# The gated embedding stage with products of rounded parts, its weights in ten pieces, and its transposes between the halves of the gate product

## The chip, the cores and the metric

The kernel runs on one core of one Trainium2 chip. The metric is the device time of one execution in microseconds (us), here the median of three. TensorE does matrix products, VectorE and ScalarE elementwise work, GpSimd the gathers, and SyncE issues DMAs.

## The reference

The whole computation is a decoder block with a mixture of experts, followed by a second block. The change touches one stage between them, the gated embedding ("ple"). There, x has 1024 rows (tokens) of 1024, p has 1024 rows of 256, `w_ple_gate` is 1024 x 1024 and `w_ple_proj` 256 x 1024, all float32:

```python
x = x + hierarchical_moe(...)
ple_gate = jax.nn.sigmoid(rms_norm(x, norm_ple[l]) @ w_ple_gate[l])
x = x + ple_gate * (p[l] @ w_ple_proj[l])
```

The sum with the experts' output is part of the stage too: each token gathers its two expert rows and adds them, weighed, to x.

## The kernel before

The kernel is a row of phases with a barrier between them. Within a phase each engine has its own instruction list, and the lists meet only at semaphores. Each list runs in its written order, so an instruction that waits holds up everything behind it on its engine.

The stage goes over eight tiles of 128 tokens. `each_tile` writes tile 0 and tile 7 out and puts tiles 1 to 6 in a loop of two tiles a pass; buffers with `b` are used in turn. What happens to tile t:

- GpSimd (L855) gathers the two expert rows of each token, `yb`, two tiles ahead.
- SyncE loads `xt` (L823) and `pt` (L824) into buffer b. The load of tile t+2 stands behind the store of tile t (L828), and the store waits for `added` of tile t.
- VectorE `weigh` (L893): adds the two weighed expert rows to `xt`. `norm`: ScalarE squares and sums (L865), VectorE takes the mean (L901), ScalarE the root (L867), VectorE the reciprocal (L904) and `h`, the scaled rows (L907).
- TensorE `turn` (L940, L943): eight transposes of h and two of pt into PSUM banks 0 to 2.
- VectorE `copy`: pT (L912), and hT with the gain (L913).
- TensorE `product` (L949) twice: the gate (eight steps of 128 rows by two halves of 512 columns, banks 4 and 5) and the projection (two steps by two halves, banks 6 and 7). Both in plain float32, which the profile shows as two records for each product. A product is "halved" by output columns: `h` is the outer loop, `k` the inner one.
- ScalarE takes the sigmoid of the gate's sums (L874). VectorE multiplies it with the projection (m, L922) and adds xt (y, L925); that sets `added`.

The orders in the lists matter here. In the step for tile t, TensorE does the gate product of t, `turn` of t+1, and the projection of t (which waits for `added` of t-1). VectorE does `norm` and `copy` of t+1, and then m and y of t. ScalarE does the square and root of t+1, then the sigmoid of t. All weights are fetched once, the gate's in one DMA of 4 MB (L835) and the projection's in one of 1 MB (L837); TensorE waits for both before the first product.

The other stages that the prediction draws on: "mix" mixes the branches, with plain products (L736) and transposes (L717) of the same shapes; "fin" is the last stage, whose products already go in rounded parts (L1122), with weights rounded on ScalarE (L1067) and the remainders on VectorE (L1104).

## Time and profile before

| | |
|---|---|
| three runs | 3751.92, 3756.41, 3767.01 us |
| median | 3756.41 us |
| profiled execution, its own time | 3761.07 us |
| its span, first to last instruction | 3759.3 us |
| mean granted clock of TensorE | 0.894 of full |
| the stage's first DMA issue | 2167.85 us |
| first transpose | 2188.16 us |
| first product of the gate | 2196.60 us |
| first transposes of tiles 1, 2, 7 | 2212.63, 2231.82, 2328.00 us |
| end of the last y | 2352.55 us |
| next stage's first DMA issue | 2356.23 us |

Times inside the profile count from the start of the span. A view of the timeline gives start, duration, engine, line, operation, output and inputs, how many instructions are merged in the row, and in brackets how long the engine was idle before it and what ended that. "PE" is TensorE's product or transpose. Products are pipelined: the duration of one record is longer than the distance from one start to the next, so distances of starts are what counts. The granted clock is given as a share of 2.4 GHz.

### The profile page before, as it was taken

The numbers are of one execution on the slowest core, as the hardware profiler recorded it, in microseconds if no ns is written. First come the engines' busy times: TensorE is split into PE (matmuls) and PEld (weight loads), VectorE is DVE, ScalarE is ACT, GpSimd is POOL, SyncE is SP. The second block draws the span as 40 slices with busy tenths as digits, with TensorE's granted clock in tenths as the row PEclk, the third lists the DMA queues.
The fourth block names the chain that finished last, engine by engine and source line by source line (L and its number), as shares of the span: only waits on it lengthen the run. The fifth ranks groups of instructions, "written<-read, shape, count | busy, mean of one in ns | idle before, by whom it ended". The sixth has DMA issues, their size and how long they took to land. (4 is left out here: it accounts for less than half of the span.)

```text
span 3759.3 us, 53218 instructions
## 1 busy us (share of the span) xinstructions
PE 3102.9 (83%) x20841; PEld 2514.8 (67%) x20841; DVE 1870.1 (50%) x2424; ACT 1196.4 (32%) x1698; POOL 684.5 (18%) x363
## 2 busy tenths in 40 slices
PE   7999948888686998399999969799998946635699
PEld 6999937777453444388888734699998745533387
DVE  3003726666363223588888723300576745566421
ACT  2000014333353111377777612201111642222310
POOL 3232224332000000222222110222221411100000
PEclk9999978888697998699999989899998967766899
DMA  4223231110203521599999742434566230021321
GB/s 169 79 98 131 106 106 45 44 47 8 77 12 139 191 101 55 205 389 399 399 399 399 291 169 78 173 104 154 177 225 211 100 137 0 0 88 33 140 95 63
DMA packets 247611, 548.22 MB, mean 146 GB/s; under 512 B 29776, under 2 KB 90576, under 8 KB 246368
## 3 DMA queue, kind: packets, MB, share of 16 engines
q1 hardware_dynamic: 198208, 431.01, 31.9%
q10 hardware_dynamic: 39376, 80.81, 5.8%
q0 software_dynamic: 9872, 34.23, 2.4%
q8 instruction: 109, 1.79, 0.2%
q14 instruction: 46, 0.38, 0.0%
HBM read 430.32 MB, written 114.50 MB: 145 GB/s over the span
## 5 line engine op out<-in xcount | busy, mean ns | idle before, releaser
L359 PE MATMUL pin_psum<-pin_sb_w,pin_sb_hT 128*128 128x354 f32 (+1 forms) x5376 | 974.7, 343 | 23.0 <-DVE pin_sb_w L321 18.0
L359 PEld LDWEIGHTS pin_psum<-pin_sb_w,pin_sb_hT 128*128 128x128 f32 x5376 | 935.7, 189 | 59.0 <-DVE pin_sb_w L321 18.8
L3827 DVE TENSOR_TENSOR moe_sb_wlo<-moe_sb_raw,moe_sb_whi 128x2048 fp32r<-128x2048 f32 x192 | 437.9, 2287 | 93.3 <-ACT moe_sb_whi L3652 93.2
L3652 ACT ACTIVATE moe_sb_whi<-moe_sb_raw 128x2048 fp32r<-128x2048 f32 x192 | 367.3, 1916 | 134.6 <-DMA moe_sb_raw<-in_w_gate 48.9
L338 DVE TENSOR_SCALAR pin_sb_xt<-pin_psum,pin_sb_ss 128x353 f32<-128x353 f32 (+1 forms) x112 | 69.3, 625 | 496.6 <-PE pin_psum L359 496.4
L293 ACT ACTIVATE pin_sb_xt<-pin_psum,pin_sb_ss 128x353 f32<-128x353 f32 (+1 forms) x112 | 64.0, 589 | 563.6 <-PE pin_psum L359 560.2
L3895 PE MATMUL moe_psum<-moe_sb_whi,moe_sb_xhi 128*128 128x512 f32 x512 | 204.6, 400 | 15.9 <-DVE moe_sb_xlo L3831 15.9
L3895 PE MATMUL moe_psum<-moe_sb_wlo,moe_sb_xhi 128*128 128x512 f32 x512 | 201.3, 393 | 0.0
L3895 PE MATMUL moe_psum<-moe_sb_whi,moe_sb_xlo 128*128 128x512 f32 x512 | 201.3, 393 | 0.0
L250 POOL CAST pin_sb_w<-pin_sb_raw 128x2832 fp32r<-128x2832 f32 (+1 forms) x26 | 75.6, 2908 | 642.8 <-PE pin_psum L359 596.3
L252 POOL TENSOR_TENSOR pin_sb_w<-pin_sb_raw,pin_sb_w 128x2832 fp32r<-128x2832 f32 (+1 forms) x26 | 185.6, 7139 | 3.9 <-issue 0.6
L3895 PEld LDWEIGHTS moe_psum<-moe_sb_whi,moe_sb_xhi 128*128 128x128 f32 x512 | 97.3, 190 | 41.3 <-issue 19.1
L3626 POOL COPY moe_sb_idx<-moe_sb_idx_all 128x1 int32 (+1 forms) x32 | 50.9, 1592 | 381.1 <-PE moe_psum L3884 378.9
L949 PE MATMUL ple_psum<-ple_sb_wg,ple_sb_hT 128*128 128x512 f32 x256 | 113.5, 602 | 6.1 <-DMA ple_sb_wp<-in_w_ple_proj 6.1
L736 PE MATMUL mix_psum<-mix_sb_wo,mix_sb_mT 128*128 128x512 f32 x256 | 113.1, 600 | 0.0
L3895 PEld LDWEIGHTS moe_psum<-moe_sb_whi,moe_sb_xlo 128*128 128x128 f32 x512 | 97.3, 190 | 20.8
L3895 PEld LDWEIGHTS moe_psum<-moe_sb_wlo,moe_sb_xhi 128*128 128x128 f32 x512 | 97.3, 190 | 19.4
L3895 PE MATMUL moe_psum<-moe_sb_whi,moe_sb_ahi 128*128 128x512 f32 x256 | 103.4, 404 | 6.4 <-DVE moe_sb_alo L3835 6.4
L1122 PE MATMUL fin_psum<-fin_sb_whi,fin_sb_mhi 128*128 128x512 f32 x256 | 101.3, 396 | 6.0 <-DVE fin_sb_mlo L1080 6.0
L3895 PE MATMUL moe_psum<-moe_sb_whi,moe_sb_alo 128*128 128x512 f32 x256 | 101.2, 395 | 0.0
L3895 PE MATMUL moe_psum<-moe_sb_wlo,moe_sb_ahi 128*128 128x512 f32 x256 | 101.1, 395 | 0.0
L1122 PE MATMUL fin_psum<-fin_sb_wlo,fin_sb_mhi 128*128 128x512 f32 x256 | 100.6, 393 | 0.0
(668 smaller groups left out, 5553.7 us busy)
## 6 DMA issues: line engine op xcount, KB each, us to landing
moe_sb_raw<-in_w_gate SPq DMA_DIRECT2D x64, 1024.0 KB, 13.9
moe_sb_raw<-in_w_up SPq DMA_DIRECT2D x64, 1024.0 KB, 14.1
moe_sb_raw<-in_w_down SPq DMA_DIRECT2D x64, 1024.0 KB, 13.1
pin_sb_raw<-in_w_in SPq DMA_DIRECT2D x16, 1412.0 KB, 8.0
scratch_proj<-pin_sb_xt ACTq DMA_DIRECT2D x16, 1412.0 KB, 7.0
pin_sb_raw<-in_w_in SPq DMA_DIRECT2D x12, 1792.0 KB, 7.8
scratch_proj<-pin_sb_xt ACTq DMA_DIRECT2D x12, 1792.0 KB, 6.3
scratch_ybuf<-moe_sb_yb ACTq DMA_DIRECT2D x32, 512.0 KB, 6.8
```

Of the source, the lines that this page charges most:

```text
L250: pool.tensor_copy(wt[b][0][:, :, :], raw[b][:, :, :])
L252: pool.tensor_tensor(wt[b][1][:, :, :], raw[b][:, :, :], wt[b][0][:, :, :].bitcast(F32), ALU.subtract)\
L293: a.activation(og[b][:, t, :], ps[:, t, 0:width], ACT.Copy, scale=ss[:, 3, t:t + 1]).then_inc(act_free, 1)
L338: v.tensor_scalar(og[b][:, t, :], ps[:, t, 0:width], ss[:, 3, t:t + 1], None, ALU.mult).then_inc(dve_free, 1)
L359: mm = te.matmul(ps[:, t, 0:cols], hT[a_part][:, k, t * P:(t + 1) * P], wt[b][w_part][:, k, :], start=(k == 0 and n == 0), stop=(k == KD - ...
L736: mm = te.matmul(ps[:, 6 + n, :], mT[:, k, :], wo[:, k, n * 512:(n + 1) * 512], start=(k == 0), stop=(k == KD - 1))
L949: mm = te.matmul(ps[:, bank + h, :], a[:, k, :], w[:, k, h * 512:(h + 1) * 512], start=(k == 0), stop=(k == n_k - 1))
L1122: mm = te.matmul(ps[:, 4 + 2 * b + h, :], m[:, k, :], w[:, k, h * 512:(h + 1) * 512], start=(k == 0 and i == 0), stop=(k == KM - 1 and i = ...
L3626: pool.tensor_copy(idx[b][:, :], idx_all[:, bass.ds(n, 1)] if not isinstance(n, int) else idx_all[:, n:n + 1])
L3652: s.activation(whi[q][:, :, :], raw[q][:, :, :], ACT.Copy).then_inc(hi, 1)
L3827: tt(wlo[q][:, :, :], raw[q][:, :, :], whi[q][:, :, :].bitcast(F32), ALU.subtract).then_inc(lo, 1)
L3895: mm = te.matmul(out, xp[:, k, :], wp[q][:, w_at, :], start=(first and i == 0), stop=(last and i == 2))
```

## The change

Four edits, all in this stage:

- Every product a @ w becomes three, hi(a) hi(w) + hi(a) lo(w) + lo(a) hi(w), in the rounded format float32r. hi is the value rounded to that format, lo what remains. The rows' hi parts are made by ScalarE (`round_rows`), after VectorE's gain (`gained`); the lo parts by VectorE after that. The same tiles are double-buffered.
- The weights arrive in ten pieces of 128 rows (eight of the gate, two of the projection), each with a semaphore, ahead of the load of tile 1. ScalarE rounds each piece (`round_weights`), VectorE takes the remainder (`rest_of_weights`): six of them ahead of the norm of tile 0, four behind it.
- For tile 0 the gate product goes by k, each step waiting for its piece.
- From tile 1 on, `turn` of the next tile stands between the two halves of the gate product instead of behind it.

```diff
@@ -786,11 +786,12 @@
 
 
 
+    KW, LEAD = KD + 2, 6
     with Phase(nc, "ple") as ph:
         ident = ph.sb("ident", [P, P])
         gcol = ph.sb("gcol", [P, KD])
-        wg = ph.sb("wg", [P, KD, D])
-        wp = ph.sb("wp", [P, 2, D])
+        raw = ph.sb("raw", [P, KW, D])
+        whi, wlo = (ph.sb(n, [P, KW, D], F32R) for n in ("whi", "wlo"))
         two = lambda n, shape: [ph.sb(f"{n}{b}", shape) for b in range(2)]
         xt = two("xt", [P, D])
         pt = two("pt", [P, 2, P])
@@ -798,7 +799,8 @@
         ss = two("ss", [P, 4])
         h = ph.sb("h", [P, D])
         hT = ph.sb("hT", [P, KD, P])
-        pT = two("pT", [P, 2, P])
+        hThi, hTlo = ([ph.sb(f"{n}{b}", [P, KD, P], F32R) for b in range(2)] for n in ("hThi", "hTlo"))
+        pThi, pTlo = ([ph.sb(f"{n}{b}", [P, 2, P], F32R) for b in range(2)] for n in ("pThi", "pTlo"))
         sg = ph.sb("sg", [P, D])
         m = ph.sb("m", [P, D])
         y = two("y", [P, D])
@@ -806,12 +808,14 @@
         wts = ph.sb("wts", [P, 2, NT])
         yb = [[ph.sb(f"yb{b}{k}", [P, D]) for k in range(2)] for b in range(2)]
         ps = ph.psum()
-        const_in, table_in, wg_in, wp_in = (ph.sem(n) for n in ("const_in", "table_in", "wg_in", "wp_in"))
+        const_in, table_in, w_hi, w_lo = (ph.sem(n) for n in ("const_in", "table_in", "w_hi", "w_lo"))
+        w_in = [ph.sem(f"w_in{k}") for k in range(KW)]
         y_in = [ph.sem(f"y_in{b}") for b in range(2)]
         weighed = ph.count("weighed")
         x_in, y_st = ([ph.sem(f"{n}{b}") for b in range(2)] for n in ("x_in", "y_st"))
-        squared, mean, root, normed, turned, copied, gate_sums, proj_sums, gates, added = (ph.count(n) for n in (
-            "squared", "mean", "root", "normed", "turned", "copied", "gate_sums", "proj_sums", "gates", "added"))
+        squared, mean, root, normed, turned, gained, rounded, copied, gate_sums, proj_sums, gates, added = (
+            ph.count(n) for n in ("squared", "mean", "root", "normed", "turned", "gained", "rounded", "copied",
+                                  "gate_sums", "proj_sums", "gates", "added"))
         blk = ph.block()
 
         @blk.sync
@@ -832,9 +836,10 @@
             load(0, 0)
             for dst, src in ((ident[:, :], g["ident"]), (gcol[:, :], g["norm_ple"].rearrange("(k p) -> p k", p=P))):
                 sp.dma_start(dst, src, allow_slow_non_contiguous=True).then_inc(const_in, 16)
-            sp.dma_start(wg[:, :, :], g["w_ple_gate"].rearrange("(k p) n -> p k n", p=P)).then_inc(wg_in, 16)
+            for k in range(KW):
+                src = g["w_ple_gate"][k * P:(k + 1) * P, :] if k < KD else g["w_ple_proj"][(k - KD) * P:(k - KD + 1) * P, :]
+                sp.dma_start(raw[:, k, :], src).then_inc(w_in[k], 16)
             load(1, 1)
-            sp.dma_start(wp[:, :, :], g["w_ple_proj"].rearrange("(k p) n -> p k n", p=P)).then_inc(wp_in, 16)
             with sp.Fori(0, NT // 2 - 1) as j:
                 for b in range(2):
                     store(2 * j + b, b)
@@ -866,16 +871,31 @@
                 s.wait_ge(mean.sem, mean.done(t))
                 s.activation(ss[b][:, 2:3], ss[b][:, 1:2], ACT.Sqrt).then_inc(root.sem, 1)
 
+            def round_rows(t, b):
+                s.wait_ge(gained.sem, gained.done(t))
+                s.activation(hThi[b][:, :, :], hT[:, :, :], ACT.Copy)
+                s.activation(pThi[b][:, :, :], blocks(ps, 2, 2), ACT.Copy).then_inc(rounded.sem, 1)
+
+            def round_weights(k):
+                s.wait_ge(w_in[k], 16)
+                s.activation(whi[:, k, :], raw[:, k, :], ACT.Copy).then_inc(w_hi, 1)
+
             def body(t, b, n):
                 if not last(t):
                     norm(t + 1, 1 - b, n + b)
+                    round_rows(t + 1, 1 - b)
                 s.wait_ge(gate_sums.sem, gate_sums.done(t))
                 s.wait_ge(added.sem, added.done(t - 1))
                 s.activation(sg[:, :], banks(ps, 4), ACT.Sigmoid).then_inc(gates.sem, 1)
 
-            for c in (squared, root, gates):
+            for c in (squared, root, rounded, gates):
                 c.begin(s)
+            for k in range(LEAD):
+                round_weights(k)
             norm(0, 0, 0)
+            for k in range(LEAD, KW):
+                round_weights(k)
+            round_rows(0, 0)
             each_tile(s, body)
 
         @blk.vector
@@ -909,8 +929,15 @@
             def copy(t, b, n):
                 ve.drain()
                 ve.wait_ge(turned.sem, turned.done(t))
-                ve.tensor_copy(pT[b][:, :, :], blocks(ps, 2, 2))
-                tt(hT[:, :, :], blocks(ps, 0, 8), bcast(gcol[:, :], P), ALU.mult).then_inc(copied.sem, 1)
+                tt(hT[:, :, :], blocks(ps, 0, 8), bcast(gcol[:, :], P), ALU.mult).then_inc(gained.sem, 1)
+                ve.drain()
+                ve.wait_ge(rounded.sem, rounded.done(t))
+                tt(hTlo[b][:, :, :], hT[:, :, :], hThi[b][:, :, :].bitcast(F32), ALU.subtract)
+                tt(pTlo[b][:, :, :], blocks(ps, 2, 2), pThi[b][:, :, :].bitcast(F32), ALU.subtract).then_inc(copied.sem, 1)
+
+            def rest_of_weights(k):
+                ve.wait_ge(w_hi, k + 1)
+                tt(wlo[:, k, :], raw[:, k, :], whi[:, k, :].bitcast(F32), ALU.subtract).then_inc(w_lo, 1)
 
             def body(t, b, n):
                 if not last(t):
@@ -924,11 +951,15 @@
                 ve.wait_ge(y_st[b], 16 * n + 16)
                 tt(y[b][:, :], xt[b][:, :], m[:, :], ALU.add).then_inc(added.sem, 1)
 
-            for c in (mean, normed, copied, added, weighed):
+            for c in (mean, normed, gained, copied, added, weighed):
                 c.begin(ve)
+            for k in range(LEAD):
+                rest_of_weights(k)
             ve.wait_ge(const_in, 32)
             ve.wait_ge(table_in, 32)
             norm(0, 0, 0)
+            for k in range(LEAD, KW):
+                rest_of_weights(k)
             copy(0, 0, 0)
             each_tile(ve, body)
 
@@ -943,28 +974,44 @@
                     mm = te.transpose(block_of(ps, 2, i), pt[b][:, i, :], ident[:, :])
                 mm.then_inc(turned.sem, 1)
 
-            def product(bank, a, w, n_k):
-                for h in range(2):
-                    for k in range(n_k):
-                        mm = te.matmul(ps[:, bank + h, :], a[:, k, :], w[:, k, h * 512:(h + 1) * 512],
-                                       start=(k == 0), stop=(k == n_k - 1))
+            def product(bank, a, b, k0, n_k, h, k):
+                hi, lo = a
+                for i, (m, w) in enumerate(((hi[b], whi), (hi[b], wlo), (lo[b], whi))):
+                    mm = te.matmul(ps[:, bank + h, :], m[:, k, :], w[:, k0 + k, h * 512:(h + 1) * 512],
+                                   start=(k == 0 and i == 0), stop=(k == n_k - 1 and i == 2))
                 return mm
+
+            gate_rows, proj_rows = (hThi, hTlo), (pThi, pTlo)
 
             def body(t, b, n):
                 te.wait_ge(copied.sem, copied.done(t))
                 te.wait_ge(gates.sem, gates.done(t - 1))
-                product(4, hT, wg, KD).then_inc(gate_sums.sem, 1)
-                if not last(t):
+                if first(t):
+                    for k in range(KD):
+                        te.wait_ge(w_lo, k + 1)
+                        for h in range(2):
+                            mm = product(4, gate_rows, b, 0, KD, h, k)
+                    mm.then_inc(gate_sums.sem, 1)
+                    te.wait_ge(w_lo, KW)
                     turn(t + 1, 1 - b, n + b)
+                else:
+                    for k in range(KD):
+                        product(4, gate_rows, b, 0, KD, 0, k)
+                    if not last(t):
+                        turn(t + 1, 1 - b, n + b)
+                    for k in range(KD):
+                        mm = product(4, gate_rows, b, 0, KD, 1, k)
+                    mm.then_inc(gate_sums.sem, 1)
                 te.wait_ge(added.sem, added.done(t - 1))
-                product(6, pT[b], wp, 2).then_inc(proj_sums.sem, 1)
+                for h in range(2):
+                    for k in range(2):
+                        mm = product(6, proj_rows, b, KD, 2, h, k)
+                mm.then_inc(proj_sums.sem, 1)
 
             for c in (turned, gate_sums, proj_sums):
                 c.begin(te)
             te.wait_ge(const_in, 32)
             turn(0, 0, 0)
-            te.wait_ge(wg_in, 16)
-            te.wait_ge(wp_in, 16)
             each_tile(te, body)
```

## Rows read from the trace of the kernel before

**Rows 1.** Stretches from transpose to transpose, tiles 1 to 7: busy us (records) by engine, clock, DMA

```profile
2231.82:2250.91 19.09, 18.48 (x51) 8.57 (x51) 7.64 (x9) 5.34 (x7) 1.88 (x2) 1.00 0.34 116
...
sum 115.37, PE 110.83 PEld 51.34 DVE 45.85 ACT 29.45 POOL 7.52; mean PE 18.47 PEld 8.56 DVE 7.64 ACT 4.91 POOL 1.25
```

**Rows 2.** Timeline of TensorE in the stage.

```profile
2212.63 1.04 PE L940 MATMUL ple_psum<-ple_sb_ident,ple_sb_h 128*128 128x128 f32 x8
...
2217.16 13.90 PE L949 MATMUL ple_psum<-ple_sb_wg,ple_sb_hT 128*128 128x512 f32 x32
2231.82 1.10 PE L940 MATMUL ple_psum<-ple_sb_ident,ple_sb_h 128*128 128x128 f32 x8 [0.77 <-DVE ple_sb_h L907]
...
2232.97 3.60 PE L949 MATMUL ple_psum<-ple_sb_wp,ple_sb_pT 128*128 128x512 f32 x8
...
2250.91 1.09 PE L940 MATMUL ple_psum<-ple_sb_ident,ple_sb_h 128*128 128x128 f32 x8 [0.61 <-DVE ple_sb_h L907]
```

**Rows 3.** Timeline of VectorE, tile 1's m and y to tile 3's h.

```profile
2236.68 1.22 DVE L922 TENSOR_TENSOR ple_sb_m<-ple_sb_sg,ple_psum 128x1024 f32<-128x1024 f32 x1 [1.95 <-PE ple_psum L949]
2238.06 1.23 DVE L925 TENSOR_TENSOR ple_sb_y<-ple_sb_xt,ple_sb_m 128x1024 f32<-128x1024 f32 x1 [0.16 <-issue]
...
2244.39 1.28 DVE L893 SCALAR_TENSOR_TENSOR ple_sb_xt<-ple_sb_yb,ple_sb_wts,ple_sb_xt 128x1024 f32<-128x1024 f32 x1 [5.11 <-DMA ple_sb_pt<-in_p]
...
2248.34 0.15 DVE L901 TENSOR_SCALAR ple_sb_ss<-ple_sb_ss 128x1 f32<-128x1 f32 x1 [1.22 <-ACT ple_sb_junk L865]
...
2250.10 0.75 DVE L907 TENSOR_SCALAR ple_sb_h<-ple_sb_xt,ple_sb_ss 128x1024 f32<-128x1024 f32 x1
```

**Rows 4.** Timeline of TensorE, the last stage's first products in rounded parts.

```profile
3555.80 0.80 PE L1122 MATMUL fin_psum<-fin_sb_whi,fin_sb_mhi 128*128 128x512 f32 x1 [6.04 <-DVE fin_sb_mlo L1080]
...
3559.70 0.39 PE L1122 MATMUL fin_psum<-fin_sb_whi,fin_sb_mhi 128*128 128x512 f32 x1
...
3562.42 0.39 PE L1122 MATMUL fin_psum<-fin_sb_whi,fin_sb_mhi 128*128 128x512 f32 x1
```

**Rows 5.** Timeline of TensorE, a restart in the mixing stage.

```profile
1468.47 1.97 PE L717 MATMUL mix_psum<-mix_sb_ident,mix_sb_h 128*128 128x128 f32 x8 [3.27 <-DVE mix_sb_h L657]
1470.23 15.79 PE L736 MATMUL mix_psum<-mix_sb_wo,mix_sb_mT 128*128 128x512 f32 x32
```

**Rows 6.** Stretch of that restart.

```profile
1468.47:1474.00 5.53, 5.53 (x13) 3.44 (x14) 1.23 (x1) 0.00 (x0) 0.00 (x0) 0.50 0.23 95
```

**Rows 7.** Instructions of the last stage's weight tile: ns min/median/max, first and last start, forms.

```profile
L1067 ACT ACTIVATE fin_sb_whi<-fin_sb_y x4: 1047/1056/1061, 3540.9 to 3557.3; 128x1024 fp32r<-128x1024 f32 x4
L1104 DVE TENSOR_TENSOR fin_sb_wlo<-fin_sb_y,fin_sb_whi x4: 1216/1222/1225, 3541.9 to 3559.1; 128x1024 fp32r<-128x1024 f32 x4
```

**Rows 8.** Groups by line in the stage: busy us, mean ns, idle before, what ended it.

```profile
L913 DVE TENSOR_TENSOR ple_sb_hT<-ple_psum,ple_sb_gcol 128x1024 f32<-128x1024 f32 x8 | 9.7, 1214 | 0.0
...
L874 ACT ACT_TABLE_LOAD x7 | 9.0, 1283 | 1.3 <-PE ple_psum L949 1.3
...
L874 ACT ACTIVATE ple_sb_sg<-ple_psum 128x1024 f32<-128x1024 f32 x8 | 8.2, 1027 | 30.5 <-PE ple_psum L949 30.4
...
L912 DVE COPY ple_sb_pT<-ple_psum 128x256 f32<-128x256 f32 x8 | 3.4, 424 | 25.5 <-PE ple_psum L943 25.5
```

**Rows 9.** Groups by line of ScalarE: a copy of 256 columns from PSUM.

```profile
L1959 ACT ACTIVATE att_sb_qkT<-att_psum 128x256 f32<-128x256 f32 x28 | 10.5, 376 | 0.0
```

**Rows 10.** Timeline of the opening, VectorE and TensorE.

```profile
2181.63 2.66 DVE L893 SCALAR_TENSOR_TENSOR ple_sb_xt<-ple_sb_yb,ple_sb_wts,ple_sb_xt 128x1024 f32<-128x1024 f32 x2 [27.01 <-DMA ple_sb_yb<-scratch_ybuf,ple_sb_di]
...
2187.26 0.75 DVE L907 TENSOR_SCALAR ple_sb_h<-ple_sb_xt,ple_sb_ss 128x1024 f32<-128x1024 f32 x1
...
2196.60 16.19 PE L949 MATMUL ple_psum<-ple_sb_wg,ple_sb_hT 128*128 128x512 f32 x32 [6.07 <-DMA ple_sb_wp<-in_w_ple_proj]
```

**Rows 11.** Stretch of the opening.

```profile
2185.00:2190.00 5.00, 1.84 (x9) 1.87 (x10) 1.07 (x3) 1.96 (x4) 1.44 (x2) 0.50 1.02 409
```

**Rows 12.** Timeline of the stage's end, TensorE and VectorE.

```profile
2328.00 1.09 PE L940 MATMUL ple_psum<-ple_sb_ident,ple_sb_h 128*128 128x128 f32 x8 [0.80 <-DVE ple_sb_h L907]
...
2351.32 1.23 DVE L925 TENSOR_TENSOR ple_sb_y<-ple_sb_xt,ple_sb_m 128x1024 f32<-128x1024 f32 x1
```

## The prediction, made before the changed kernel ran

> **What bounds the stage now.** The change touches one stage, the gated embedding, so I read that stage alone. First the stretches view, cut at the first transpose of each tile: six tile turns take 115.37 us, 19.23 us each, at full clock (1.00, 2.4 GHz), and TensorE is recorded busy for 110.83 of them [rows 1]. That looks like a TensorE bound, and a cheaper product would then pay in full. The timeline says otherwise. After 13.90 us of gate product TensorE still waits 0.6 to 0.9 us in every turn before it can transpose, and VectorE's h is what it waits for [rows 2]. So I followed h back on VectorE [rows 3]: the multiply m of tile t-1 starts at 2236.68, y ends at 2239.29, then comes a wait of 5.11 us for a DMA (SyncE reloads xt and pt of tile t+1 into the buffers of t-1, and does so only behind the store of y, which waits for `added`), then the two weighing operations, the mean, the root, and h (start 2250.10, 0.75 us). The transpose follows at 2250.91. The ring is: transposes, projection product, m, y, reload, weighing, norm, transposes of the next tile. Its two parts are
>
> - from the first transpose to m: 2231.82 to 2236.68, 4.86 us (1.15 us of ten transposes, 3.43 of projection, 0.28 of the last product's tail and hand-over) [rows 2, 3];
> - from m to the next first transpose: 2250.91 - 2236.68 = 14.23 us; over the six turns 19.23 - 4.85 = 14.38 us. I use 14.38.
>
> The gate product (32 records a tile, 2217.16 to the end of the queue at about 2230.9) lies beside the second part, and covers it all but those 0.6 to 0.9 us. It is not in the ring. The ring is what the change must be priced on.
>
> **Part 1, the products.** A 128x512 product in plain f32 is two records, 13.90 us for 32 records: about 0.86 us for one product [rows 2]. In rounded parts it is three records. In the last stage the same form goes at 3559.70 to 3562.42 for 12 of them: 0.227 us each, 0.68 for three [rows 4]. Gate: 48 records, 10.88 us instead of 13.7. Projection: 12 records, 2.72 instead of 3.43. If all eight tiles paid in full, 8 x 3.5 = 28 us would go. The Trainium skill ("TensorE: Matmul & The Clock Gate", section "Wait — 56ns, not 53.3ns?") has 215.7 ns from start to start for 512 columns at full clock; the row's 227 ns is longer, and the row decides. By the page's figure the sum below would be an estimated 3 us smaller.
>
> **Part 2, where the transposes stand.** From tile 1 on, PE does half the gate product, then waits for h(t+1) and transposes, then the other half, then the projection. Of the ring's two parts the second is untouched: m, y, the store, the reload, weighing and norm are the same instructions in the same order. But it is now covered by only one half, 24 x 0.227 = 5.44 us. And the other half moves into the first part, between the transposes and m:
>
> - first part, at full clock: 1.15 + 5.44 + 2.72 + 0.27 = 9.58 us, instead of 4.85;
> - the new turn: 9.58 + 14.38 = 23.96 us, instead of 19.23;
> - TensorE's idle stretch: the first half ends at 9.3 + 5.44 = 14.7 us after the transposes began, the next begin at 24: some 9 us, where there are 0.6 to 0.9 now.
>
> Beside this part lies: gain (1.21 us) [rows 8], the rounding on ScalarE (1.06 us for 1024 columns [rows 7]; 0.38 for 256 [rows 9]), the remainders on VectorE (1.22 [rows 7] and, from the copy of the same shape, 0.42 [rows 8]). From the transposes' end at 1.35 they are done at about 5.9, before the projection is (9.3), so the next first half does not wait for them. VectorE's queue holds m behind them, and ScalarE's queue holds the sigmoid behind the rounding, but both need the second half (6.6) anyway. The sigmoid after it, with its table load (1.28 + 1.03) [rows 8], ends at about 9.1, level with the projection. Cost nothing; were the projection faster by 0.5 us, the sigmoid would be last.
>
> **Part 3, the clock.** After an idle stretch the trace shows TensorE at half clock. In the branch mixing stage 3.27 us of idle are followed by eight transposes of 1.97 us, and by 15.79 us for a product that takes 13.90 at full clock [rows 5, 2]; the granted clock is 0.50 (1.2 GHz) for those 5.53 us [rows 6]. In this stage, after 6.07 us idle, the first product takes 16.19 [rows 10], 2.3 more. In the last stage, after 6.04 us, nine rounded products take 3.90 us where 2.04 would do [rows 4]. A 9 us gap will do the same in each turn. Price of a 5.5 us spell from the first transpose: ten transposes 1.15 us longer, then 3.2 us of product at 0.43 instead of 0.227 us, 1.5 us lost. Together 2.65. Bounds: 0 if the clock stays up; 1.9 for a spell of 3.9 us; 3.2 if transposes leave it low and the products begin their own spell of 4.4 us. I take 2.65, the only row in which transposes and product follow each other after idle time. The new turn: 26.6 us, 7.4 more than now.
>
> The Trainium skill speaks against this edit (same page, section "Loop structure matters more than you think"): a loop nest that puts a long wait between bursts of matmuls starts each burst at the low clock. The rows of the mixing stage agree (3.27 us idle, then 0.50). By the rule the sum is the one below, without it that of the second rival.
>
> **Part 4, the opening.** Now: weighing starts at 2181.63, h ends 6.4 us later, and the first product starts at 2196.60, held by the weights' DMA; the transposes of tile 1 start at 2212.63 [rows 10, 2]. Afterwards ten pieces of 0.52 MB arrive one behind the other on SyncE's queue. Ahead of and beside the sixth some 6 MB must move, at the 0.4 MB/us that the DMA engines run at there [rows 11]: it is there at about 2186, the tenth at about 2191. VectorE's queue puts the remainders of six pieces ahead of the weighing of tile 0: rounding 1.06 and remainder 1.22 [rows 7] end at about 2188.4, h 6.4 us later at 2194.8, four more remainders (ScalarE rounds them from 2193.8 on) at 2199.6, then gain, rounding and remainders of the rows, 4.5 us. First product at about 2204.1, 7.5 us later than now. It takes 10.88 + 1.86 (the low clock, [rows 4]) = 12.7 instead of 16.0, so tile 1's transposes start at 2216.9: **+4.3 us**. Bounds for the start: not before 2196.6 less some 3 us if the pieces' work is all hidden, and 2208 if they come slower. The reload of tile 1 is issued behind ten issues instead of one, but its data are wanted only at about 2204.
>
> Tile 0's turn is different: no second half. m(0) waits for the sigmoid, which stands in ScalarE's queue behind the rounding of tile 1's rows: 1.35 + 1.21 + 1.06 + 0.38 + 1.28 + 1.03, m at about 6.55 us instead of 4.80. **+1.7 us**.
>
> **Part 5, the tail.** From the transposes of tile 7 (2328.00) to the end of the last y (2352.55) it is 24.55 us now [rows 12]. Then: 1.15 + 5.44 + 2.72 + 10.88 + 2.72 + 2.65 + 0.27, and 2.53 for m and y, = 28.36. **+3.8 us**: the second half of tile 6, now behind the transposes, outweighs what the two tiles' products save.
>
> **Sum.** 4.3 + 1.7 + 5 turns x 7.4 (36.9) + 3.8 = +46.7 us. The profiled execution took 3761.07 us (span 3759.3), 4.7 above the median of 3756.41. Against its own time it is 3807.8; against the median, 3803.
>
> **Rivals.**
> - *TensorE is the bound, and the time falls.* For it: 110.83 of 115.37 us busy. It decides at the second part of the ring: only if m to transpose fitted behind the first half (about 5.2 us instead of 14.38) would the turn be TensorE's own 14.75 us, tile 0's turn about 12, and the sum 4.3 - 7.3 - 22.4 + 1.2 = -24 us, 3732. Already below 9.65 us the turn would be no longer than now. Against it: the reload alone is 5.1 us, the two weighings 2.7, square, table load and h another 4, none of them changed; and PE waits even behind a whole gate product. Chance 0.03.
> - *The clock stays at 2.4 GHz through the gaps.* Less 6 x 2.65 and 1.86: +28.9 us, 3785. Against it: the three restarts above, all after shorter idle time. 0.07.
> - *The clock stays low for the whole burst* after each gap: 1.15 us and 36 products x 0.2 = 8.35 a turn instead of 2.65. 5.7 x 6 = 34 more: +81, 3837. For it: a burst is only some 15 us between gaps; against it: no spell above lasts over 5.6 us. 0.06.
> - *The change gives back in the opening what it loses* (pieces start the products before all weights are in): it can't, since the row remainders stand behind all ten pieces in VectorE's queue; at best 10 us less, about 3793. 0.04.
>
> **How the numbers follow.** Forecast as summed, 0.80: 3803 us. Its bounds (spell of 1.9 to 3.2 us, opening -8 to +4, runs differing by 5) make 3790 to 3813; reaching into the two clock rivals, 3784 to 3818. 0.5% is 19 us, about what a measurement of this kernel tells from no change; only the first rival is faster (0.03), and something unseen of over 28 us would be needed for "same" (0.02). Slower: 0.95.
>
> **What would show it.** In the changed kernel's stage: rounded products 0.227 us apart; first transposes some 26 us apart; before each, about 9 us of TensorE idle ended by h (against 0.6 to 0.9); the transposes at half clock, about 2.3 us for ten; VectorE's wait for pt still about 5.1 us; m waiting on a TensorE product or the sigmoid some 12 us after the transposes began; first product at about 2204. It is wrong if h comes earlier after m than 14.4 us, if TensorE keeps its clock over the gaps, or if the stage's turns are under 20 us.

## The result, and the profile after

| | before | changed |
|---|---|---|
| median of six runs | 3760.43 us | 3805.82 us |
| lowest, highest | 3751.92, 3767.01 | 3803.75, 3817.58 |
| profiled execution, its own time | 3761.07 | 3805.35 |
| its span | 3759.3 | 3803.6 |
| stage: its first DMA issue to that of the next stage | 188.38 | 237.72 |

Changed to before: 1.013, 95% interval 1.011 to 1.015. The six runs of the kernel before are the three on record and three more. The kernel became 45 us slower; forecast were 47 (3803 us, or 3807.8 against the profiled execution).

The stage alone grew by 49.3 us. The changed kernel's profiled execution reached it 9.5 us earlier (2158.31 against 2167.85 us), over code that the change doesn't touch, and took 4.5 us more after it. No cause is known for these 5 us outside the stage: the nine profiled executions of this document reached the stage between 2157.6 and 2172.2 us, over the same code, and a kernel's times spread by some 14 us from one execution to the next. So the stage's length is the sharper measure, and it is the one used below for steps.

The changed kernel's page, span and TensorE's line (busy time, share of the span, instructions). Over the whole kernel TensorE is busy 11 us less than before (3102.9), and the kernel is slower all the same:

```profile
span 3803.6 us, 53600 instructions
...
PE 3091.6 (81%) x21001; PEld 2557.9 (67%) x21001; DVE 1889.4 (50%) x2442; ACT 1216.3 (32%) x1724; POOL 685.4 (18%) x363
```

Stretches from transpose to transpose, columns as in [rows 1]: first the one that begins with tile 1's transposes (the prediction calls it tile 0's turn, as it ends tile 0's work), then three of the other five, then the sum of all six:

```profile
2209.53:2230.17 20.64, 9.91 (x48) 7.61 (x46) 8.87 (x10) 6.27 (x8) 1.87 (x2) 0.88 0.25 84
2230.17:2256.75 26.58, 17.85 (x71) 14.29 (x71) 8.87 (x10) 6.27 (x8) 1.87 (x2) 0.82 0.24 83
2256.75:2282.46 25.71, 16.63 (x70) 13.52 (x71) 8.88 (x10) 6.27 (x8) 1.87 (x2) 0.83 0.27 89
...
2335.70:2362.72 27.02, 17.98 (x71) 14.39 (x71) 8.87 (x10) 6.27 (x8) 0.00 (x0) 0.82 0.13 44
sum 153.19, PE 97.45 PEld 78.06 DVE 53.24 ACT 37.64 POOL 7.49; mean PE 16.24 PEld 13.01 DVE 8.87 ACT 6.27 POOL 1.25
```

Six turns take 153.19 us, where there were 115.37 [rows 1]. TensorE is recorded busy for 97.45 of them, so 56 us are idle, against 5 before. The granted clock is 0.82 or 0.83 in the last five and 0.88 in the first, where it was 1.00.

One turn on TensorE, to be set beside [rows 2]:

```profile
2230.17 1.97 PE L971 MATMUL ple_psum<-ple_sb_ident,ple_sb_h 128*128 128x128 f32 x8 [8.51 <-DVE ple_sb_h L927]
2231.93 0.64 PE L974 MATMUL ple_psum<-ple_sb_ident,ple_sb_pt 128*128 128x128 f32 x2
2232.21 0.78 PE L980 MATMUL ple_psum<-ple_sb_whi,ple_sb_hThi 128*128 128x512 f32 x1
...
2235.73 0.39 PE L980 MATMUL ple_psum<-ple_sb_whi,ple_sb_hTlo 128*128 128x512 f32 x1
...
2247.63 0.40 PE L980 MATMUL ple_psum<-ple_sb_whi,ple_sb_hTlo 128*128 128x512 f32 x1
2256.75 1.97 PE L971 MATMUL ple_psum<-ple_sb_ident,ple_sb_h 128*128 128x128 f32 x8 [8.73 <-DVE ple_sb_h L927]
```

TensorE waits 8.51 and 8.73 us for h instead of 0.6 to 0.9. The ten transposes take 2.04 us (2230.17 to 2232.21) instead of 1.15, at half clock. The products go at half clock until 2235.7, and from there 0.233 us apart (2235.73 to 2247.63 holds 51 distances).

The same turn on VectorE, to be set beside [rows 3]:

```profile
2242.53 1.22 DVE L949 TENSOR_TENSOR ple_sb_m<-ple_sb_sg,ple_psum 128x1024 f32<-128x1024 f32 x1 [5.75 <-PE ple_psum L980]
2243.91 1.23 DVE L952 TENSOR_TENSOR ple_sb_y<-ple_sb_xt,ple_sb_m 128x1024 f32<-128x1024 f32 x1 [0.16 <-issue]
2250.23 1.28 DVE L913 SCALAR_TENSOR_TENSOR ple_sb_xt<-ple_sb_yb,ple_sb_wts,ple_sb_xt 128x1024 f32<-128x1024 f32 x1 [5.09 <-DMA ple_sb_pt<-in_p]
...
2254.18 0.15 DVE L921 TENSOR_SCALAR ple_sb_ss<-ple_sb_ss 128x1 f32<-128x1 f32 x1 [1.22 <-ACT ple_sb_junk L870]
...
2255.94 0.75 DVE L927 TENSOR_SCALAR ple_sb_h<-ple_sb_xt,ple_sb_ss 128x1024 f32<-128x1024 f32 x1
```

From m (2242.53) to the next transposes (2256.75) it is 14.22 us; it was 14.23. Nothing in that part of the ring changed, its DMA wait (5.09, before 5.11) included. From the transposes (2230.17) to m it is 12.36 us where it was 4.86. These 7.5 us are the whole loss of this turn.

The opening, ScalarE (the rounding of the sixth piece), VectorE and then TensorE, beside [rows 10]:

```profile
2177.72 1.06 ACT L881 ACTIVATE ple_sb_whi<-ple_sb_raw 128x1024 fp32r<-128x1024 f32 x1 [0.38 <-DMA ple_sb_raw<-in_w_ple_gate]
```

```profile
2178.81 1.23 DVE L940 TENSOR_TENSOR ple_sb_wlo<-ple_sb_raw,ple_sb_whi 128x1024 fp32r<-128x1024 f32 x1 [0.21 <-ACT ple_sb_whi L881]
2180.22 2.66 DVE L913 SCALAR_TENSOR_TENSOR ple_sb_xt<-ple_sb_yb,ple_sb_wts,ple_sb_xt 128x1024 f32<-128x1024 f32 x2 [0.18 <-issue]
...
2185.85 0.75 DVE L927 TENSOR_SCALAR ple_sb_h<-ple_sb_xt,ple_sb_ss 128x1024 f32<-128x1024 f32 x1
2186.55 4.63 DVE L940 TENSOR_TENSOR ple_sb_wlo<-ple_sb_raw,ple_sb_whi 128x1024 fp32r<-128x1024 f32 x4
...
2195.04 0.42 DVE L936 TENSOR_TENSOR ple_sb_pTlo<-ple_psum,ple_sb_pThi 128x256 fp32r<-128x256 f32 x1
```

```profile
2195.51 0.80 PE L980 MATMUL ple_psum<-ple_sb_whi,ple_sb_hThi 128*128 128x512 f32 x1 [6.40 <-DVE ple_sb_pTlo L936]
...
2209.53 1.03 PE L971 MATMUL ple_psum<-ple_sb_ident,ple_sb_h 128*128 128x128 f32 x8
```

Counted from the stage's first DMA issue (2158.31), the weighing starts after 21.9 us (before: 13.8) and the first product after 37.2 (before: 28.8). The weighing stands behind six pieces, and the sixth was there only after 19.4 us. The product of tile 0 takes 14.0 us instead of 16.0.

The end of the stage, TensorE and VectorE, beside [rows 12]:

```profile
2362.72 1.97 PE L971 MATMUL ple_psum<-ple_sb_ident,ple_sb_h 128*128 128x128 f32 x8 [9.04 <-DVE ple_sb_h L927]
```

```profile
2390.63 1.23 DVE L952 TENSOR_TENSOR ple_sb_y<-ple_sb_xt,ple_sb_m 128x1024 f32<-128x1024 f32 x1
```

From the last transposes to the end of the last y it is 29.14 us; it was 24.55.

### The profile page after: what moved, and what is told of

Its sections match the earlier page's. It is cut to its first block and busy times, and to the rows that moved or that the text cites. A ratio compares the mean times of both kernels' runs of the same rounds, so it can differ in the third digit from the quotient of the medians.

```text
span 3803.6 us, 53600 instructions
## 1 busy us (share of the span) xinstructions
PE 3091.6 (81%) x21001; PEld 2557.9 (67%) x21001; DVE 1889.4 (50%) x2442; ACT 1216.3 (32%) x1724; POOL 685.4 (18%) x363
## 5 line engine op out<-in xcount | busy, mean ns | idle before, releaser
L3942 PEld LDWEIGHTS moe_psum<-moe_sb_whi,moe_sb_xhi 128*128 128x128 f32 x512 | 97.3, 190 | 41.7 <-issue 19.4
L1169 PE MATMUL fin_psum<-fin_sb_whi,fin_sb_mlo 128*128 128x512 f32 x256 | 101.0, 394 | 0.0
## 6 DMA issues: line engine op xcount, KB each, us to landing
moe_sb_raw<-in_w_gate SPq DMA_DIRECT2D x64, 1024.0 KB, 13.9
```

Source lines behind the costliest of these rows:

```text
L1169: mm = te.matmul(ps[:, 4 + 2 * b + h, :], m[:, k, :], w[:, k, h * 512:(h + 1) * 512], start=(k == 0 and i == 0), stop=(k == KM - 1 and i = ...
L3942: mm = te.matmul(out, xp[:, k, :], wp[q][:, w_at, :], start=(first and i == 0), stop=(last and i == 2))
```

## The experiments

Each ran on the chip beside the kernel before. "Turn" is the mean of the five turns between the first transposes of tiles 2 and 7, in the profiled execution. The ratio is to the kernel before, run beside them: its median was 3760.37 us beside the first four experiments and 3762.80 beside the last three.

| kernel | median us | ratio, 95% interval | stage us | turn us |
|---|---|---|---|---|
| before | 3760.43 | | 188.38 | 19.24 |
| changed | 3805.82 | 1.013, 1.011 to 1.015 | 237.72 | 26.51 |
| turn_behind | 3776.30 | 1.0042, 1.0028 to 1.0056 | 207.12 | 21.34 |
| turn_amid_plain | 3810.56 | 1.0134, 1.0117 to 1.0151 | 243.93 | 28.44 |
| filler | 3790.51 | 1.009, 1.007 to 1.0109 | 227.89 | 24.77 |
| early_reload | 3769.39 | 1.0028, 1.0018 to 1.0037 | 200.87 | 20.51 |
| norm_ahead | 3739.67 | 0.9926, 0.9909 to 0.9943 | 167.76 | 15.11 |
| opening | 3727.46 | 0.9903, 0.9888 to 0.9918 | 157.38 | 15.11 |
| plain_norm_ahead | 3753.82 | 0.9971, 0.9958 to 0.9985 | 183.12 | 18.26 |

The theory: a ring of transposes, (second half,) projection, m, y, reload, weighing and norm sets the turn, and the half of the product that was put into it is the loss. First rival: the rounded products or the pieces lose the time (turn_behind, turn_amid_plain). Second rival: the clock is no part of it, and the ring has its length at any clock (filler). Third rival: TensorE or another engine sets the turn, and the reload is only what it happens to wait for (early_reload).

**turn_behind.** One part of the change undone:

```diff
                 else:
-                    for k in range(KD):
-                        product(4, gate_rows, b, 0, KD, 0, k)
-                    if not last(t):
-                        turn(t + 1, 1 - b, n + b)
-                    for k in range(KD):
-                        mm = product(4, gate_rows, b, 0, KD, 1, k)
+                    for h in range(2):
+                        for k in range(KD):
+                            mm = product(4, gate_rows, b, 0, KD, h, k)
                     mm.then_inc(gate_sums.sem, 1)
+                    if not last(t):
+                        turn(t + 1, 1 - b, n + b)
```

> The changed kernel, but the transposes of the next tile again stand behind the whole gate product; rounded products and ten pieces stay. Theory (the ring: transposes, second half, projection, m, y, reload, norm sets the turn): the second half leaves the first part of the ring. m then waits for the sigmoid, which stands behind the rounding of the rows in ScalarE's queue (about 6.3 us after the transposes begin), so a turn is 6.3 + 14.5 = 20.8 us, with TensorE idle some 3.2 us before the transposes, and up to 2 us more where that drops its clock. The stage is 14 to 27 us longer than in the kernel before, 22 to 35 shorter than in the changed one (49.3 longer than before). Rival (the rounded products or the pieces themselves cost the time, for instance by TensorE's own work): turns stay near 26 us and the kernel near 3806.

Its stretches, then one wait on VectorE, then one on TensorE:

```profile
2224.00:2244.79 20.79, 15.52 (x71) 12.11 (x70) 8.87 (x10) 6.27 (x8) 1.88 (x2) 1.00 0.26 82
2244.79:2265.93 21.14, 15.56 (x70) 12.12 (x70) 8.87 (x10) 6.28 (x8) 1.88 (x2) 1.00 0.32 105
...
2308.64:2330.61 21.97, 18.38 (x70) 14.51 (x71) 8.87 (x10) 6.27 (x8) 0.00 (x0) 0.86 0.23 79
```

```profile
2249.91 0.42 DVE L936 TENSOR_TENSOR ple_sb_pTlo<-ple_psum,ple_sb_pThi 128x256 fp32r<-128x256 f32 x1
2251.10 1.22 DVE L949 TENSOR_TENSOR ple_sb_m<-ple_sb_sg,ple_psum 128x1024 f32<-128x1024 f32 x1 [0.78 <-ACT ple_sb_sg L889]
```

```profile
2265.93 1.09 PE L971 MATMUL ple_psum<-ple_sb_ident,ple_sb_h 128*128 128x128 f32 x8 [3.28 <-DVE ple_sb_h L927]
```

The stage is 18.7 us longer than before and 30.6 shorter than in the changed kernel. m starts 6.31 us after the transposes (2244.79 to 2251.10), behind the sigmoid: the price of rounding on ScalarE in its queue, as expected. An idle stretch of 3.0 to 3.3 us stands before the transposes of tiles 2 to 7. Of the turns behind such a stretch one kept its clock (1.00), and the lowest had 0.86, which is 1 us of the turn. So the placement of the transposes is about 31 of the stage's 49 us. The other 18.7 stay with the rounding and the pieces: 7.0 in the opening, 1.6 in tile 0's turn and 10.5 in the five turns, less 0.4 at the end. Of the 10.5, the rounding ahead of the sigmoid (m at 6.31 instead of 4.86 us) is some 7; that the rest is the clock and small differences is worked out, not tested.

**turn_amid_plain.** The same part alone, on the kernel before (with hT in two buffers for it, not shown):

```diff
-                product(4, hT, wg, KD).then_inc(gate_sums.sem, 1)
-                if not last(t):
-                    turn(t + 1, 1 - b, n + b)
+                if first(t):
+                    product(4, hT[b], wg, KD).then_inc(gate_sums.sem, 1)
+                    turn(t + 1, 1 - b, n + b)
+                else:
+                    product(4, hT[b], wg, KD, (0,))
+                    if not last(t):
+                        turn(t + 1, 1 - b, n + b)
+                    product(4, hT[b], wg, KD, (1,)).then_inc(gate_sums.sem, 1)
```

> The kernel before (plain f32 products, weights in two DMAs) with the one edit that from tile 1 on the transposes of the next tile stand between the two halves of the gate product (hT in two buffers for that). Theory (the ring): first part 1.15 + 6.86 + 3.43 + 0.28 = 11.7 us, second 14.4, TensorE idle some 7 us, its clock down after it (2.6 us): turns of 26 to 29 us, the last turn's tail about 9 us longer, the kernel about 45 to 57 us slower than before. Rival (the placement is harmless, rounding or pieces lose the time): turns of 19 us, the kernel as before, near 3760.

```profile
2212.84:2232.30 19.46, 11.56 (x35) 5.46 (x33) 7.64 (x9) 3.66 (x5) 1.87 (x2) 0.90 0.27 87
2232.30:2260.02 27.72, 19.99 (x51) 9.80 (x51) 7.64 (x9) 6.00 (x7) 1.87 (x2) 0.87 0.24 80
...
sum 161.67, PE 114.65 PEld 55.63 DVE 45.84 ACT 29.44 POOL 7.48; mean PE 19.11 PEld 9.27 DVE 7.64 ACT 4.91 POOL 1.25
```

The placement alone makes the kernel 50 us slower, with no rounding and no pieces in it. Beside turn_behind this settles the first rival for the turns: with the placement taken away 31 us of the loss go, and put in alone it brings 50. The rival keeps a smaller part: turn_behind, with rounding and pieces but without the placement, is still 16 us slower than the kernel before. The placement costs more here than in the changed kernel (9.2 against 7.3 us a turn), as a plain half (6.86 us) is longer than a rounded one (5.6), and as the rounded projection gives back 0.6.

**filler.** Work for nothing in the gap, to hold the clock:

```diff
                     if not last(t):
+                        for i in range(30):
+                            te.matmul(ps[:, 3, :], hThi[b][:, i % KD, :], whi[:, i % KD, 0:512], start=True, stop=True)
                         turn(t + 1, 1 - b, n + b)
```

> The changed kernel with 30 more rounded products into an unused PSUM bank between the first half of the gate product and the transposes, from tile 1 to 6: about 7 us of TensorE work in a gap of 9, for nothing but its clock. Theory (the low clock after the gap costs some 2.2 us a turn): granted clock 1.00 through the turn, ten transposes 1.2 instead of 2.3 us, turns of about 24.3 instead of 26.5 us; the stage 10 to 14 us shorter although TensorE does 180 products more. Rival (the clock has no part in it, the turn is the ring's length at any clock): turns stay at 26.5 us, the kernel at 3806, or longer where the filler delays the transposes.

Three of its stretches (TensorE's busy time holds the filler), and the transposes at the start of the first and of the third:

```profile
2229.63:2253.87 24.24, 22.31 (x100) 17.75 (x100) 8.86 (x10) 6.28 (x8) 1.87 (x2) 1.00 0.27 92
2253.87:2278.41 24.54, 22.31 (x100) 17.89 (x101) 8.87 (x10) 6.28 (x8) 1.87 (x2) 1.00 0.28 91
2278.41:2304.57 26.16, 23.87 (x101) 18.95 (x101) 8.87 (x10) 6.28 (x8) 1.87 (x2) 0.93 0.26 85
```

```profile
2229.63 1.09 PE L971 MATMUL ple_psum<-ple_sb_ident,ple_sb_h 128*128 128x128 f32 x8 [1.67 <-DVE ple_sb_h L927]
...
2278.41 1.09 PE L971 MATMUL ple_psum<-ple_sb_ident,ple_sb_h 128*128 128x128 f32 x8 [2.22 <-DVE ple_sb_h L927]
```

180 more products make the kernel 15 us faster than the changed one (medians 3790.51 and 3805.82), the stage 9.8. Where the clock held (1.00), a turn takes 24.2 to 24.5 us, 2.1 less than 26.51. In one of the five turns it fell all the same (0.93), behind 2.2 us of idle time and the transposes, and that turn is 26.16. It fell in the same way behind tile 7's transposes. So the clock's share is 2.1 us of a turn, and the other 5.2 of the 7.3 are there at full clock. The stage's gain is just under the 10 to 14 us that were expected; without these two spells, some 1.6 us each, it would be some 13.

**early_reload.** The reload taken out of the ring. The loops over the tiles are written out for it on SyncE, ScalarE, VectorE and TensorE; SyncE's part and the buffers:

```diff
-        xt = two("xt", [P, D])
-        pt = two("pt", [P, 2, P])
+        xt = [ph.sb(f"xt{b}", [P, D])[:, :] for b in range(2)] + [raw[:, i, :] for i in range(2)]
+        pt = [ph.sb(f"pt{b}", [P, 2, P])[:, :, :] for b in range(2)] + [
+            raw[:, 2 + i, 0:2 * P].rearrange("p (a c) -> p a c", c=P) for i in range(2)]
...
-            with sp.Fori(0, NT // 2 - 1) as j:
-                for b in range(2):
-                    store(2 * j + b, b)
-                    load(2 * j + b + 2, b)
+            sp.wait_ge(w_lo, 4)
+            load(2)
+            load(3)
+            for t in range(NT):
+                store(t, t % 2)
+                if t + 4 < NT:
+                    load(t + 4)
```

> The changed kernel with four buffers for xt and pt instead of two (the two further ones lie in the raw weights, free after the split), so that a tile is loaded two turns earlier and its load no longer stands behind the store of y; the loop over the tiles is written out for that. Theory (the reload is a link of the ring): VectorE's wait of 5.1 to 5.6 us for pt goes, the part from m to the transposes is 9.5 instead of 14.5 us, turns of about 21.5 us (19.3 if the shorter idle stretch of some 4 us leaves the clock up), the kernel 25 to 43 us faster than the changed one, 3763 to 3781. Rival (TensorE or another engine sets the turn, the reload is only what it happens to wait for): turns within 1 us of 26.5, the kernel near 3806.

VectorE from m to the next h, and one stretch:

```profile
2264.61 1.22 DVE L954 TENSOR_TENSOR ple_sb_m<-ple_sb_sg,ple_psum 128x1024 f32<-128x1024 f32 x1 [5.31 <-PE ple_psum L986]
2265.90 1.23 DVE L957 TENSOR_TENSOR ple_sb_y<-ple_sb_raw,ple_sb_m 128x1024 f32<-128x1024 f32 x1
2267.29 2.64 DVE L918 SCALAR_TENSOR_TENSOR ple_sb_xt<-ple_sb_yb,ple_sb_wts,ple_sb_xt 128x1024 f32<-128x1024 f32 x2 [0.16 <-issue]
...
2272.90 0.75 DVE L932 TENSOR_SCALAR ple_sb_h<-ple_sb_xt,ple_sb_ss 128x1024 f32<-128x1024 f32 x1
```

```profile
2253.21:2273.71 20.50, 16.89 (x70) 13.58 (x71) 8.87 (x10) 6.28 (x8) 1.87 (x2) 0.92 0.33 110
```

The weighing now follows y within 0.16 us. From m (2264.61) to the transposes (2273.71) it is 9.10 us instead of 14.5: the wait of 5.1 to 5.6 us is gone. The written-out loops give little of it (y starts 1.29 us after m, in the changed kernel 1.38). The turn fell by 6.0 us and the kernel by 36. TensorE's instructions and their order were not touched, so TensorE's work did not set the turn: the link that was cut did. The clock is 0.92 after idle stretches of 3.6 us: m starts 11.4 us after the transposes, 9.8 at full clock in filler, so that the turn is 20.5 and not some 18.9.

**norm_ahead.** early_reload, with the rest of the ring opened: norm of tile t+2 ahead of m and y of tile t (VectorE's part is shown), with the sigmoid ahead of that norm on ScalarE:

```diff
                 if not last(t):
-                    norm(t + 1, 1 - b, n + b)
                     copy(t + 1, 1 - b, n + b)
+                if t + 2 < NT:
+                    norm(t + 2, b, n + 1)
                 ve.drain()
                 ve.wait_ge(gates.sem, gates.done(t))
```

> The kernel with four buffers (early_reload; rounded products, transposes between the halves), and on VectorE and ScalarE the weighing and norm of tile t+2 ahead of m and y of tile t instead of behind them. Theory (the ring): h is ready a turn before its transposes, so TensorE goes from product to product: 11.2 for the gate, 1.15 for ten transposes, 2.8 for the projection, turns of 15.2 us at full clock instead of 20.5; the rounding of the rows lies beside the second half. The kernel about 28 us faster than with early reload alone (3769), 3741, and faster than the kernel before by some 19. Rival (VectorE becomes the bound: copy 4.3, weighing and norm 6.5, m and y 2.6, with its waits on ScalarE for square, table load, root and rounding): turns of 17 to 18 us, about 3754.

```profile
2229.68:2244.83 15.15, 15.15 (x71) 12.39 (x71) 10.36 (x12) 6.28 (x8) 1.87 (x2) 1.00 0.54 181
2244.83:2259.93 15.10, 15.10 (x72) 12.33 (x70) 9.83 (x11) 6.28 (x8) 1.87 (x2) 1.00 0.46 154
...
sum 87.61, PE 85.46 PEld 69.30 DVE 53.23 ACT 36.38 POOL 7.49; mean PE 14.24 PEld 11.55 DVE 8.87 ACT 6.06 POOL 1.25
```

TensorE has no gap left in these turns: 15.10 us a turn, 72 records, clock 1.00. So the placement that costs 50 us in the ring costs TensorE nothing outside it. That it now even hides the rounding of the rows is likely but not tested, as no run has the open ring with the transposes behind the whole rounded product. In tile 0's turn, where no second half follows the transposes, TensorE waits 1.48 us for the rows' remainders:

```profile
2223.14 0.50 PE L994 MATMUL ple_psum<-ple_sb_whi,ple_sb_hThi 128*128 128x512 f32 x1 [1.48 <-DVE ple_sb_pTlo L947]
```

**plain_norm_ahead.** What the products are worth by themselves: buffers and order of norm_ahead on the kernel before (there, four buffers of their own, transposes behind the whole product, and the sigmoid ahead of the norm).

> The kernel before (plain f32 products, weights in two DMAs, transposes behind the whole gate product), with four buffers and the norm two tiles ahead as in norm_ahead. Theory: here TensorE's own work was only just hidden by the ring, so freeing the ring gives no more than TensorE's wait of 0.6 to 0.9 us a turn: turns of 18.3 us instead of 19.2, about 5 us faster than before, 3755. Set beside norm_ahead it tells what the rounded products are worth once the ring is open: 18.3 - 15.2 = 3.1 us a turn. Rival (most of the gain of norm_ahead is from the reordering, not the products): more than 10 us faster than before.

```profile
2234.40:2252.66 18.26, 18.26 (x52) 8.64 (x51) 7.64 (x9) 4.94 (x6) 1.88 (x2) 1.00 0.38 123
...
sum 109.56, PE 109.56 PEld 51.88 DVE 45.86 ACT 29.66 POOL 7.51; mean PE 18.26 PEld 8.65 DVE 7.64 ACT 4.94 POOL 1.25
```

18.26 us a turn with no idle time, against 15.10: the rounded products save 3.16 us a turn, near the 3.5 that they were worth on paper, once TensorE is the bound. The reordering alone gives the kernel before 9 us at the median (3762.80 to 3753.82, with an interval of 6 to 16) and 5.3 in the stage (188.38 to 183.12); the expected value was 5. So of norm_ahead's 23 us the reordering is 9, and the rounded products with their pieces and placement are 14 (3753.82 to 3739.67); in the stage it is 5.3 and 15.4.

**opening.** norm_ahead with the opening reordered:

```diff
-    KW, LEAD = KD + 2, 6
+    KW, LEAD, MID = KD + 2, 2, 4
...
-            for k in range(LEAD, KW):
+            for k in range(LEAD, MID):
                 rest_of_weights(k)
             copy(0, 0, 0)
+            for k in range(MID, KW):
+                rest_of_weights(k)
             norm(1, 1, 0)
```

(and the same on ScalarE, with `round_rows(0, 0)` between).

> The same as norm_ahead, with the opening in another order: two pieces of the weights split ahead of the norm of tile 0 (instead of six), two behind it, then the rounding of tile 0's rows, and only then the other six pieces. Theory (the opening's 6.4 us come from VectorE's queue: six pieces ahead of the weighing, all ten ahead of the row remainders): the weighing starts at 14 us after the stage's first DMA issue instead of 22, the first product at about 28 instead of 37, tile 1's transposes at about 42 instead of 51; 8 to 10 us faster than norm_ahead, about 3732. Rival (the arrival of the weights sets the opening): less than 3 us faster, since the last piece is there only at about 27 to 29 us, and its remainder some 2 us later.

```profile
2174.79 1.22 DVE L953 TENSOR_TENSOR ple_sb_wlo<-ple_sb_raw,ple_sb_whi 128x1024 fp32r<-128x1024 f32 x1 [1.44 <-ACT ple_sb_whi L885]
2176.20 2.66 DVE L926 SCALAR_TENSOR_TENSOR ple_sb_xt<-ple_sb_yb,ple_sb_wts,ple_sb_xt 128x1024 f32<-128x1024 f32 x2 [0.18 <-issue]
...
2188.89 0.42 DVE L949 TENSOR_TENSOR ple_sb_pTlo<-ple_psum,ple_sb_pThi 128x256 fp32r<-128x256 f32 x1
2189.22 6.89 DVE L953 TENSOR_TENSOR ple_sb_wlo<-ple_sb_raw,ple_sb_whi 128x1024 fp32r<-128x1024 f32 x6
```

```profile
2189.36 0.80 PE L998 MATMUL ple_psum<-ple_sb_whi,ple_sb_hThi 128*128 128x512 f32 x1 [4.27 <-DVE ple_sb_pTlo L949]
```

The weighing starts 13.9 us after the stage's first DMA issue (2162.31), the first product 27.0 after it; in the changed kernel these are 21.9 and 37.2. The stage is 10.4 us shorter than norm_ahead's, the median 12, against 8 to 10 expected. So the order in VectorE's queue set the opening, and the rival (the arrival of the weights, at most 3 us to be had) is out. The arrival still had a part in the changed kernel, since that order put the weighing behind the sixth piece. This is the fastest version, 35 us faster than the kernel before (3762.80 to 3727.46).

## Why the prediction was right, step by step

| step, as forecast | forecast us | measured us |
|---|---|---|
| opening, to the transposes of tile 1 | +4.3 | +6.4 (44.78 to 51.22 after the stage began) |
| tile 0's turn | +1.7 | +1.45 (19.19 to 20.64) |
| five turns | +36.9 | +36.4 (96.18 to 132.55) |
| tail | +3.8 | +4.6 (24.55 to 29.14) |
| leaving the stage | 0 | +0.5 |
| sum | +46.7 | +49.3 |

The stage grew by 2.6 us more than forecast, and yet the kernel by 1 us less (medians, 45 against 47), because the profiled executions differ by 5 us the other way outside the stage. That the kernel's own figure came out this near is luck.

- *The ring.* Forecast: the part from m to transposes stays 14.4, the other goes from 4.85 to 12.2 us with the clock. Measured: 14.5 and 12.0, means of five. early_reload and norm_ahead show that it is a ring and not a coincidence: each link taken out shortens the turn (the reload by 6.0 us: 5.4 from m to the transposes, 0.6 of the clock's price), until TensorE's own 15.1 us is reached.
- *TensorE as the bound.* The rival's signs (110.83 of 115.37 us busy [rows 1]) were real: TensorE's own work was 18.26 us a turn (plain_norm_ahead), 5% below the ring's 19.24. But the ring set the turn, so a cheaper gate product alone had nothing to give, and an open ring alone gives 1 us. Both together give 4.1 (19.24 to 15.11).
- *The clock.* Forecast 2.65 us a turn; filler gives 2.1. The turn shown fits the forecast: its half-clock spell lasted 5.6 us from the first transpose and cost 2.5 (m at 12.36 us, 9.82 at full clock in filler). But the spells differ: in the five turns they lasted 5.6, 2.9, 4.6, 5.2 and 5.9 us (the turn from 2256.75 had its products at full clock from 2259.7). So as a mean the term was a quarter too large.
- *The products.* Forecast 0.227 us each, from [rows 4]; measured 0.233. 36 of them lie in a turn's first part: 0.24 us, which goes against the clock's error and hides half of it in the turn's length. That, too, is luck. In the tail there are 96: 0.6 of the 0.8 us that it was short. The prediction's side estimate for products closer together (3 us) is 3.7 by its own terms, as 324 products lie on the path (48, 180 and 96); they came out farther apart.
- *The opening.* This is the term that was most off, 2.1 us. The order was right (VectorE's queue, first product forecast at 36.3 us after the stage began, measured 37.2, by [rows 10] 28.8 before). The sixth piece came later than forecast, after 19.4 instead of some 18 us. The product itself was priced too low: 12.7 us, measured 14.0 (2195.51 to 2209.53). Its half-clock spell lasted 6.1 us and 14 products (to 2201.59), where the forecast took the 9 products and 3.9 us of [rows 4], and the rest went at 0.233. The rival of a clock that stays low argued that no spell lasts over 5.6 us; this one did, but it ended, and so did all others.
- *What was costed at nothing* stayed hidden: the rows' remainders were done 6.6 us after the transposes began (2236.78), and m waited for a product till 12.4 (the wait of 5.75 us that TensorE ended). The reload of tile 1, issued behind the ten pieces, held nobody.

## What to carry to other kernels

A share of busy time near one does not make an engine the bound: follow what it waits for, even where the wait is only 0.7 us, since a ring that is just that much longer than the engine's work may lie behind it. Before moving work within an engine's queue, ask on which side of the ring's wait it comes to stand: a half product between transposes and m adds its whole length to every turn, and the same half beside the reload adds nothing as long as the reload's side of the ring is the longer one. When a product is made cheaper, open the ring first (a third and fourth buffer for the reload, the norm two tiles ahead); with the ring open the same edit went from 45 us slower to 14 faster than the plain kernel with its ring open (23 faster than the kernel before), and with the opening in order to 35 faster than the kernel before.

## What the runs showed of the hardware that was not expected

- Three rounded products on the same shapes take 0.700 us in this stage at full clock (0.233 each, in the changed kernel and in all its variants), against 0.680 (0.227) in the last stage [rows 4]. Buffers and their strides differ between the two stages, and other things may; no run told them apart, and the cause is open. Over the 480 products of the stage it is some 3 us.
- TensorE's clock fell after idle stretches of 3.0 to 3.3 us in four of the five turns that follow one in turn_behind (1.00, 0.92, 0.90, 0.86, 0.92 by turn), and twice behind 2.2 us (filler, before the transposes of tiles 4 and 7; 2.3 us before those of tile 5 kept it). With 8.5 to 9.2 us of idle time it fell every time. In filler such a short gap cost nothing or 1.6 us, and it was not always the same one.
- Transposes at full clock don't tell that the products behind them have it. In filler the transposes from 2278.41 took 1.09 us for eight, as at full clock, and the products from 2279.58 went at half clock (granted clock 0.50 from 2279.8 to 2282), 0.43 us apart.
